# The level products of an HGRN2 chunk in one core's kernel: f32 operands, or 16-bit heads and remainders

## What is computed

```python
b = jnp.cumsum(gc, axis=1)                       # gc = log f, per key channel
diff = b[:, :, None] - b[:, None, :]
dec = jnp.where(mask, jnp.exp(jnp.where(mask, diff, 0.0)), 0.0)
A = jnp.einsum('bthk,btshk,bshk->bhts', qc, dec, kc)
o = (jnp.einsum('bhts,bshv->bthv', A, vc)
     + jnp.einsum('bthk,bhkv->bthv', qc * jnp.exp(b), S))
bl = b[:, -1]
S = (jnp.exp(bl)[..., None] * S
     + jnp.einsum('bshk,bshv->bhkv', kc * jnp.exp(bl[:, None] - b), vc))
```

## Time and profile before

| | |
|---|---|
| median of 3 runs | 1023.69 us (1023.05 to 1025.93) |
| the profiled execution: span, first to last instruction | 1026.3 us |
| PE, weight loads, DVE, ACT, POOL busy | 984.2, 714.3, 582.0, 430.0, 161.0 us |
| level products (L462, L464, L469), PE busy | 16.9, 80.4, 10.9 + 7.1 us |
| mean granted clock of PE | 0.981 |

### The profile page before, as it was taken

How to read it: one execution, slowest core, us unless ns; L and a number is a source line. 1 busy time by engine, 2 the same in 40 slices (tenths; PEclk the granted TensorE clock), 3 DMA queues, 4 the chain that set the end, 5 groups by cost and what they waited for, 6 DMA issues and landing times.

```text
span 1026.3 us, 19994 instructions
## 1 busy us (share of the span) xinstructions
PE 984.2 (96%) x7423; PEld 714.3 (70%) x7478; DVE 582.0 (57%) x1652; ACT 430.0 (42%) x810; POOL 161.0 (16%) x208
## 2 busy tenths in 40 slices
PE   7899986899999999999999999999999999999987
PEld 3465875469775887579766976697759775887554
DVE  1453688436763576436754566366635773477445
ACT  2531747313651365135713373237413661345321
POOL 4000024301130112011110112011301130111212
PEclk9999998899999999999999999999999999999998
DMA  9984301100110011000110011001101010100413
GB/s 313 326 275 130 118 24 59 62 2 21 42 63 0 20 41 43 19 20 0 42 62 0 21 41 62 0 21 41 62 0 41 0 50 1 42 1 23 118 42 111
DMA packets 46590, 60.62 MB, mean 59 GB/s; under 512 B 2748, under 2 KB 40208, under 8 KB 46524
## 3 DMA queue, kind: packets, MB, share of 16 engines
q1 hardware_dynamic: 46524, 59.86, 17.8%
HBM read 48.90 MB, written 10.95 MB: 58 GB/s over the span
## 4 chain that ended last, share of the span: by engine, by line
PE 90%; DVE 5%; issue 2%; ACT 1%; DMA 1%; SPq 1%; DVEq 0%; ACTq 0%
PE ring L390 66%; PE lev L464 7%; PE aux L507 3%; PE okv L521 2%; PE lev L469 1%; PE okv L491 1%; PE lev L462 1%; PE ring L521 1%; PE okv L493 1%; PE okv L492 1%; DMA work<-in_w_in_dram 1%; PE okv L811 1%; PE aux L441 1%; PE aux L477 1%; PE aux L428 1%
## 5 line engine op out<-in xcount | busy, mean ns | idle before, releaser
L390 PE MATMUL ring<-hnh,wih 128*128 128x256 bf16 (+1 forms) x1152 | 291.1, 264 | 5.8 <-DVE hnl L1273 4.2
L390 PE MATMUL ring<-hnh,wil 128*128 128x256 bf16 (+1 forms) x1152 | 291.2, 264 | 0.0
L390 PE MATMUL ring<-hnl,wih 128*128 128x256 f16 (+1 forms) x1152 | 291.1, 264 | 0.0
L390 PE MATMUL ring<-woh,work 128*128 128x512 f16 x512 | 162.3, 379 | 1.7
L390 PEld LDWEIGHTS ring<-hnh,wih 128*128 128x128 f16 x1152 | 112.5, 100 | 18.1 <-issue 4.5
L1165 DVE TENSOR_TENSOR qq<-qq,gg 128x256 f32<-128x256 f32 x96 | 44.1, 459 | 140.1 <-PE lev L464 99.8
L390 PEld LDWEIGHTS ring<-hnl,wih 128*128 128x128 f16 x1152 | 110.6, 98 | 12.9
L390 PEld LDWEIGHTS ring<-hnh,wil 128*128 128x128 bf16 x1152 | 110.6, 98 | 12.4
L390 PE MATMUL ring<-wih,hnh 128*128 128x512 f16 (+1 forms) x264 | 101.1, 383 | 4.0 <-ACT kk L851 4.0
L390 PE MATMUL ring<-wih,hnl 128*128 128x512 f16 (+1 forms) x264 | 101.1, 383 | 1.4 <-issue 0.2
L1587 POOL TENSOR_TENSOR kk<-kk,cols 128x256 f32<-128x256 f32 x32 | 29.3, 935 | 419.3 <-ACT kk L851 419.3
(11 more groups left out here) (310 smaller groups left out, 1585.5 us busy)
## 6 DMA issues: line engine op xcount, KB each, us to landing
xin<-in_x_prompt_dram SPq DMA_DIRECT2D x16, 512.0 KB, 3.4
work<-in_x_prompt_dram SPq DMA_DIRECT2D x16, 512.0 KB, 4.3
out_dram<-work SPq DMA_DIRECT2D x16, 512.0 KB, 2.6
work<-in_ada_w_dram SPq DMA_DIRECT2D x4, 1024.0 KB, 10.4
woh<-in_ada_w_dram SPq DMA_DIRECT2D x4, 1024.0 KB, 11.8
work<-in_w_in_dram SPq DMA_DIRECT2D x4, 1024.0 KB, 7.2
woh<-in_w_in_dram SPq DMA_DIRECT2D x4, 1024.0 KB, 8.5
wol<-in_w_in_dram SPq DMA_DIRECT2D x4, 1024.0 KB, 9.6
```

The costliest lines, as they stand in the source:

```text
L390: last = mm(out, a(k), b(k), start=start and k == ks[0] and j == 0, stop=stop and k == ks[-1] and j == 2)
```

## The change

Queries and keys of every level are split as the projections' operands are, and `level` makes three 16-bit products per block: key head with query head, key head with query remainder, key remainder with query head. It does this at all levels in full width, so levels 6 and 7 no longer work in small blocks. The head of q and k is made by ACT (`q_out` for level 0, `k_head`, and `heads` for the others), the remainder of q by DVE (`operands`), the remainder of k by POOL (`k_rest`). The updates of q, k and the decays are now `carry`, and `take` only copies a level into `am`. There are two sets of operands, so those of level l are made once level l-2 is through PE; `operands(l)`, `take(l - 2)` and `carry(l)` follow each other on DVE. Only the blocks that a level changes are split again: 256 of 512 columns. The decode stage keeps its f32 products.

```diff
+        qrh, qrl = sb("qrh", [P, 2 * T], BF16), sb("qrl", [P, 2 * T], F16)
+        qhi = [sb(f"qhi{i}", [P, T], BF16) for i in range(2)]
+        qlo = [sb(f"qlo{i}", [P, T], F16) for i in range(2)]
+        khi = [sb(f"khi{i}", [P, 2 * T], F16) for i in range(2)]
+        klo = [sb(f"klo{i}", [P, 2 * T], BF16) for i in range(2)]
...
+        def k_set(l):
+            return max(l - 1, 0) % 2
+
+        def odd(t, l):
+            return blocks(t, 1 << (l - 1))[:, :, 1, :]
+
+        def even(t, l):
+            return blocks(t, 1 << (l - 1))[:, :, 0, :]
+
+        def packed(t, l):
+            return t.rearrange("p (b m) -> p b m", m=1 << (l - 1))
...
-                if l == 0:
-                    pe.wait_ge(q_sb.sem, q_sb.at(n, p + 1))
-                    pe.wait_ge(k_ok.sem, k_ok.at(n, 2 * p + 2))
-                elif l == 1:
-                    pe.wait_ge(q_f.sem, q_f.at(n, p + 1))
-                else:
-                    pe.wait_ge(q_upd.sem, q_upd.at(n, LEVELS * p + l - 1))
-                    pe.wait_ge(k_upd.sem, k_upd.at(n, LEVELS * p + l - 1))
-                m = 1 << (l - 1) if l else 0
+                pe.wait_ge(q_lo.sem, q_lo.at(n, i + 1))
+                pe.wait_ge(k_lo.sem, k_lo.at(n, LEVELS * p + max(l, 1)))
+                kh, kl = khi[k_set(l)], klo[k_set(l)]
+                qh, ql, w = (qrh, qrl, P) if l == 0 else (qhi[l % 2], qlo[l % 2], P // 2)
                 for hc in range(4):
-                    q, k = qq[:, P * hc:P * hc + P], kk[:, P * hc:P * hc + P]
-                    if l == 0:
-                        last = mm(lev[i % 2][:, P * hc:P * hc + P], k, q, start=True, stop=True)
-                    elif m < 32:
-                        last = mm(lev[i % 2][:, P // 2 * hc:P // 2 * hc + P // 2], k, blocks(q, m)[:, :, 1, :],
-                                  start=True, stop=True)
-                    else:
-                        for s in range(0, P, 2 * m):
-                            o = P // 2 * hc + s // 2
-                            last = mm(lev[i % 2][s:s + m, o:o + m], k[:, s:s + m], q[:, s + m:s + 2 * m],
-                                      start=True, stop=True)
+                    o, a, b = lev[i % 2][:, w * hc:w * hc + w], slice(P * hc, P * hc + P), slice(w * hc, w * hc + w)
+                    mm(o, kh[:, a], qh[:, b], start=True, stop=False)
+                    mm(o, kh[:, a], ql[:, b], start=False, stop=False)
+                    last = mm(o, kl[:, a], qh[:, b], start=False, stop=True)
                 last.then_inc(lev_ps.sem, 1)
...
             def q_out(n, p):
                 act.wait_ge(q_ps.sem, q_ps.at(n, p + 1))
+                A(qrh[:, :], ring[1][:, :], ACT.Copy).then_inc(q_hi.sem, 1)
                 A(qq[:, :], ring[1][:, :], ACT.Copy).then_inc(q_sb.sem, 1)
+
+            def k_head(n, p):
+                act.wait_ge(k_ok.sem, k_ok.at(n, 2 * p + 2))
+                A(khi[0][:, :], kk[:, :], ACT.Copy).then_inc(k_hi.sem, 1)
+
+            def heads(n, p, l):
+
+                if l >= 3:
+                    act.wait_ge(lev_ps.sem, lev_ps.at(n, p * (LEVELS + 1) + l - 1))
+                if l >= 2:
+                    act.wait_ge(k_upd.sem, k_upd.at(n, LEVELS * p + l - 1))
+                    A(even(khi[k_set(l)][:, :], l), even(kk[:, :], l), ACT.Copy).then_inc(k_hi.sem, 1)
+                    act.wait_ge(q_upd.sem, q_upd.at(n, LEVELS * p + l - 1))
+                else:
+                    act.wait_ge(q_f.sem, q_f.at(n, p + 1))
+                A(packed(qhi[l % 2][:, :], l), odd(qq[:, :], l), ACT.Copy).then_inc(q_hi.sem, 1)
...
+                k_head(n, 0)
                 q_out(n, 0)
                 weights("wi", 4)
+                heads(n, 0, 1)
+                heads(n, 0, 2)
                 for t in range(NT):
                     act.wait_ge(iv_ps.sem, iv_ps.at(n, t + 1))
                     A(vv[:, t, :], ring[t][:, :], ACT.Copy).then_inc(v_sb.sem, 1)
                     if t == 0:
                         weights("wi", 5)
+                    heads(n, 0, 3 + t)
+                heads(n, 0, 5)
...
+                    if t == 0:
+                        heads(n, 0, 6)
+                        heads(n, 0, 7)
...
+                k_head(n, 1)
                 q_out(n, 1)
                 weights("wi", 9, 10)
+                heads(n, 1, 1)
+                heads(n, 1, 2)
...
                 xa_out(n, 0)
                 weights("wi", 11)
+                heads(n, 1, 3)
                 ga_out(n, 0)
+                heads(n, 1, 4)
+                heads(n, 1, 5)
                 gates_out(n, 0)
                 weights("wo", 0)
                 xa_out(n, 1)
+                heads(n, 1, 6)
                 decay(n, 0)
+                heads(n, 1, 7)
                 root(n, 0)
                 ga_out(n, 1)
...
-            def take(n, p, l):
+            def level_done(n, p, l):
 
                 i = p * (LEVELS + 1) + l
                 dve.wait_ge(lev_ps.sem, lev_ps.at(n, i + 1))
+                if l:
+                    dve.wait_ge(amask.sem, amask.at(n, i))
+
+            def operands(n, p, l):
+
+                dve.wait_ge(q_hi.sem, q_hi.at(n, p * (LEVELS + 1) + l + 1))
                 if l == 0:
                     dve.wait_ge(u_ps.sem, u_ps.at(n, 2 * p))
+                    dve.wait_ge(q_sb.sem, q_sb.at(n, p + 1))
+                    V.tensor_tensor(qrl[:, :], qq[:, :], qrh[:, :], ALU.subtract).then_inc(q_lo.sem, 1)
                     dve.wait_ge(f_ok.sem, f_ok.at(n, p + 1))
                     V.tensor_tensor(qq[:, :], qq[:, :], ff[:, :], ALU.mult).then_inc(q_f.sem, 1)
-                    V.copy_predicated(am[:, :, :], eye[:, :].unsqueeze(1).to_broadcast([P, 4, P]),
-                                      lev[i % 2][:, :].rearrange("p (h t) -> p h t", h=4)).then_inc(amask.sem, 1)
                     return
-                dve.wait_ge(amask.sem, amask.at(n, i))
+                if l >= 2:
+                    level_done(n, p, l - 2)
+                V.tensor_tensor(packed(qlo[l % 2][:, :], l), odd(qq[:, :], l), packed(qhi[l % 2][:, :], l), ALU.subtract)\
+                    .then_inc(q_lo.sem, 1)
+
+            def carry(n, p, l):
+
                 m = 1 << (l - 1)
                 nb = 2 * T // (2 * m)
                 j = LEVELS * p + l
@@ -1158,14 +1212,26 @@
                     dve.wait_ge(q_f.sem, q_f.at(n, p + 1))
                 else:
                     dve.wait_ge(q_upd.sem, q_upd.at(n, j - 1))
-                    dve.wait_ge(k_upd.sem, k_upd.at(n, j - 1))
                     dve.wait_ge(g_upd.sem, g_upd.at(n, j - 1))
+                dve.wait_ge(q_lo.sem, q_lo.at(n, p * (LEVELS + 1) + l + 1))
                 g = products(m)
-                qo, ke = blocks(qq[:, :], m)[:, :, 1, :], blocks(kk[:, :], m)[:, :, 0, :]
+                qo, ke = odd(qq[:, :], l), even(kk[:, :], l)
                 V.tensor_tensor(qo, qo, g[:, :, 0:1].to_broadcast([P, nb, m]), ALU.mult).then_inc(q_upd.sem, 1)
+                dve.wait_ge(k_lo.sem, k_lo.at(n, j))
                 V.tensor_tensor(ke, ke, g[:, :, 1:2].to_broadcast([P, nb, m]), ALU.mult).then_inc(k_upd.sem, 1)
+                if p == 0 and l == LEVELS:
+                    level_done(n, 0, LEVELS - 1)
                 o = goff(2 * m)
                 V.tensor_tensor(gg[:, o:o + nb], g[:, :, 0], g[:, :, 1], ALU.mult).then_inc(g_upd.sem, 1)
+
+            def take(n, p, l):
+
+                i = p * (LEVELS + 1) + l
+                if l == 0:
+                    V.copy_predicated(am[:, :, :], eye[:, :].unsqueeze(1).to_broadcast([P, 4, P]),
+                                      lev[i % 2][:, :].rearrange("p (h t) -> p h t", h=4)).then_inc(amask.sem, 1)
+                    return
+                m = 1 << (l - 1)
                 r = m if m == P // 2 else P
...
+                operands(n, 0, 0)
                 if not first:
                     y_rest(n - 1, 0)
+                operands(n, 0, 1)
+                carry(n, 0, 1)
+                if not first:
                     y_rest(n - 1, 1)
-                    y_split(n - 1)
-                for l in range(LEVELS + 1):
-                    take(n, 0, l)
-                    if l == 0:
+                for l in range(2, LEVELS + 1):
+                    operands(n, 0, l)
+                    take(n, 0, l - 2)
+                    carry(n, 0, l)
+                    if l == 2:
                         weights(5)
+                        if not first:
+                            y_split(n - 1)
+                take(n, 0, LEVELS - 1)
+                level_done(n, 0, LEVELS)
+                if not first:
+                    m_out(n - 1, 0)
+                take(n, 0, LEVELS)
                 weights(6)
-                if not first:
-                    m_out(n - 1, 0)
                 state(n, 0, 0)
                 if not first:
                     m_out(n - 1, 1)
@@ -1339,11 +1415,18 @@
                     x_out(n - 1, 0)
                 forget(n, 1)
                 weights(9, 10)
```

(56 more changed lines are left out.)

12 lines of the change are left out of this document (10 added, 2 removed).

## The result

| | before | changed |
|---|---|---|
| median, 4 runs each on one chip | 1024.7 us (1023.05 to 1025.93) | 1037.43 us (1036.43 to 1040.0) |
| profiled execution, span | 1026.3 us | 1034.7 us |
| a middle body (first forget-gate product to the next) | 108.43 us | 109.19 us |
| first product of the second body | 186.38 | 194.54 |
| first product of the decode stage | 935.93 | 944.14 |

The ratio is 1.0123, with a 95% interval from 1.0103 to 1.0143: slower, by 12.7 us in the medians.

What follows compares the result with a forecast made beforehand. PE was taken to bound the kernel, busy 96% of the span. -50.4 (levels) + 14.0 (level 0 wait) + 18.9 (second gates wait) + 11.9 (clock) + 7.9 (first body) = +2.3 us, giving 1026 us; range 986 to 1046.

Steps and rivals of the forecast that it cites:

- Rival 3: Slower: the clock falls at level 0 and the second gates, strided POOL remainders at 0.9 us; 1041 us, chance 0.24.
- The levels: PE's twelve products take 0.35 us a level, 0.67 at level 0; saves 3.15 us a half, 50.4 over 16.
- the bound above it: Upper bound on PE's product cost, a straight line between two rows: 37 ns at 64 columns, 62 at 128.
- The first place: Level 0 at a body's start: PE waits 2.0 us for q's remainder on DVE; seven bodies, 14.0 us.
- the walk from the earlier trace: Stepping POOL, DVE and PE through a body's start in the old profile, giving the 2.0 us wait at level 0.
- The second place: Gates of the second half: PE waits 2.7 us for DVE's second convolution; seven bodies, 18.9 us.
- The clock: PE's granted clock falls after the 2.7 us gates wait, costing 1.7 us a body, 11.9 us in all.
- the 1.68 us wait in the earlier trace: Idle row in the old profile; Rival 3 decides once the level 0 wait passes it, for 2.0 is more.
- Rival 2: The waits come but the clock stays up: 1014 us, from 1004 to 1021; chance 0.20.
- The first body: Body with weight pieces and no y_head: takes back 7.9 us (4 to 12) of the saving.
- Rival 1: Waits hardly come, 1.5 us a body, with no fall of the clock: 989 us, 975 to 1004; chance 0.22.

Runs made afterwards that it cites:

- e7_one: Changed kernel, loop kept, with only the first of each level's three products (head times head), so A lacks the remainder products: 1021.62 us, one run.
- e2_unrolled: Changed kernel with all eight bodies written out on every engine, no loop: 1023.06 us, ratio 0.9956 to the kernel before.
- e5_hn: Changed kernel, loop kept, with ACT's normalised blocks and DVE's remainders and second convolution earlier, take 7 last: 1014.61 us, ratio 0.9881 to the kernel before.
- e1_conv: Changed kernel with the second convolution moved directly behind recur(0) on DVE: 1036.33 us, ratio 1.0101 to the kernel before.
- e4_gp: Changed kernel with ACT's first-body copy of the modulation gate moved ahead of the heads of levels 1 and 2: 1037.11 us, ratio 1.0109 to the kernel before.
- e8_two: Changed kernel, loop kept, with two of each level's three products (the one with the remainder of k left out): 1037.93 us, one run.
- e6_all: Kernel of e5_hn with all bodies written out and the first body's gate copy moved forward: 998.02 us, ratio 0.9715 to the kernel before.
- e10: Kernel of e6_all with ACT's ga_out(1) back ahead of hn_out(1), directly behind the root: 1001.48 us, ratio 0.9766 to the kernel before.

## Why the prediction was right in its range and wrong in its sum

Forecast was +2.3 us of span; it is +8.4. The terms, as measured in the profiled execution:

| term | forecast | measured |
|---|---|---|
| PE's levels | -50.4 | 3.15 a half, 16 halves: -50.4 |
| wait at level 0 | +14.0 | 0 |
| idle time at the loop's start | not seen | 5 x 2.13 = +10.7 |
| wait before the second gates | +18.9 | 6 x 2.89 + 2.13 = +19.5 |
| wait before level 5 | not seen | 6 x 0.43 = +2.6 |
| clock | +11.9 | 7 falls x 1.7 = +11.9 |
| first body beyond the saving | +7.9 | 8.16 + 6.3 = +14.5 |
| sum | +2.3 | +8.8 (8.4 by the spans) |

That the time still lies in the range is in part luck: a term of +14.0 that did not come stands against terms of +10.7, +2.6 and +6.6 that were missing or too small. The measured 1037.4 us is nearer to Rival 3's 1041 than to the forecast's 1026, although the wait at level 0, on which Rival 3 rests, did not come, and POOL's strided remainders took 0.76 us and not its 0.9.

**The levels** were right to the hundredth: 0.35 and 0.67 us for twelve products, or 29 ns a product of 64 columns and 56 ns one of 128. The estimate from the decode rows held, and not the bound above it, 37 and 62 ns.

**The first place** failed as a sum, not as a mechanism. In the body read above the hold is there, in DVE's and POOL's timeline:

```profile
417.84 2.01 POOL L1667 TENSOR_TENSOR work<-sil,stat 128x1024 bf16<-128x1024 f32 x1
418.01 2.38 DVE L1197 TENSOR_TENSOR qrl<-qq,qrh 128x512 f16<-128x512 f32 x1
```

The remainder is there at 420.39, and PE reaches level 0 at 420.60: 0.21 us to spare, because PE itself had lost 1.9 us at the loop's start. In e7_one, where PE does not lose them and DVE still does, the wait is 1.6 to 2.0 us in all five bodies behind a jump. Nor is the hold there every time: of the changed kernel's seven bodies it is in three (2.38 us); in the other four the remainder starts first and takes 0.68, as it does in each body of e2_unrolled, where neither engine loses time at a jump and nothing waits. So the step that failed is the walk from the earlier trace rows, which took PE's start and DVE's start in the old trace as fixed to one another: DVE's own 1.8 to 2.0 us at the jump were in it, PE's new ones were not. It also took one body, behind a jump, for all seven. The scan was held too, for which the prediction had no row: the two scans took 1.63 us beside POOL's bounds (305.73) and 2.17 beside `klo` (414.86), against 1.39 in the earlier trace rows; and the remainder took 2.38 beside y_head against 0.68.

**The loop's start** was in no case of mine. It could have been suspected from the trace of before: in five bodies DVE idled 1.8 to 2.0 us at the jump, released by "issue", and q8 had moved 27 packets in all and none from 295 to 829 us, that is in the loop behind its first turn; the change adds 120 matmuls to a loop of 712. The prediction counted what a product costs, and not how many the loop holds.

**The second place** was right, step and size: 2.73 us against 2.7. The chain was also the right one to attack: e5_hn, which takes ACT's first two normalised blocks and DVE's convolution forward in their queues, won 23 us.

**The clock** was right in sum, seven falls of 1.7 us, by luck: its reason was not. The 1.7 us that the prediction counts for a fall is what the window behind the 1.68 us wait in the earlier trace rows has lost, 6.00 x (1 - 0.72) = 1.68 us; the changed kernel's seven falls lasted 3.41 us at 0.50 each, 1.7 us again. I had tied it to the gates' wait alone, one fall each; it fell behind four of the six waits of 2.73 us, behind the one of 1.96 in the last body, and behind two of the five at the jump. The same count over the runs, from the second body on and without the last: behind a wait of 2.2 to 3.05 us before the gates or `turn_k` (the changed kernel, e1, e2, e4, e7, e8) the clock fell 29 times in 36; behind the 1.8 to 2.3 us at the jump 9 times in 30; behind a wait of 1.0 to 1.3 us (e5, e6, e10) never in 18. Nor did it fall behind the five waits of 1.64 to 1.98 us before level 0 in e7_one. So the 1.68 us of the earlier trace rows was a fair warning of a chance, not a threshold. Why e2_unrolled had only two falls behind six waits of 2.98 us is open. The falls at both level 0 and the gates of Rival 3 came in no body of the changed kernel, since level 0 did not wait; and Rival 2's clock that stays up was not seen either, each of its middle bodies holds one fall.

**The first body** was mis-sized by 6.6 us. The first half saves nothing (109.28 against 109.36 at the first product of its second half), where I had -1.4. In the second half I had 3.0 us of DVE work; PE's waits there (us):

```profile
126.94 0.29 PE L476 MATMUL lev<-qrh,khi 128*128 128x128 bf16 x1 [5.22 <-ACT gp L1040]
...
149.31 0.24 PE L476 MATMUL lev<-qhi,khi 128*128 128x64 bf16 x1 [2.99 <-DVE am L1239]
...
165.78 1.11 PE L485 MATMUL aux<-ident,kk 128*128 128x128 f32 x4 [9.56 <-DVE hnl L1339]
171.11 3.78 PE L515 MATMUL aux<-xc,wg 128*128 128x256 f32 x8 [4.21 <-DVE xc L1299]
```

The first is one that a reader of the diff could find: ACT's copy of the modulation gate, which frees the `lev` banks, had come to stand behind heads that wait for DVE. e4_gp took 3.9 us of it away and the body gave 2.8 back. How the rest divides between weight pieces, splits and the low clock was not tried.

**Rival 1**, that the waits hardly come, described what the change could be with another order of the queues and no loop: e6_all, at 998 us, lies in its range.

## What to carry to other kernels

A change that takes work off the engine that bounds the kernel is worth what the next engines' queues let through; here the same products are worth +12.7 us or -28.6 us by the order of five items on two engines and the form of the loop. Count the instructions that are added to a loop on each engine, and look in the profile for packets of the instruction queue and for idle time released by "issue" at the jump: here PE had neither in a middle body with 704 and 712 matmuls, and with 768 and 832 it had 9 packets and 1.8 to 2.3 us. When a wait is moved, look at the instruction in front of the one that waited: it may want the same thing.

## What the hardware showed that was not expected

- With a loop of 712 matmuls on TensorE (the kernel before) q8 moved no packet in a middle body; with one of 768 (e8_two) it moved 9, 0.15 MB, and TensorE stood still for 2.0 to 2.2 us at the jump, in four of five bodies with 1.1 to 1.5 us more behind it. The straight code here had no such idle time: the longest one released by "issue" there was 0.7 us (e1_conv, decode stage). Why the longer loop's instructions are moved in every turn and the shorter one's are not, no run shows.
- VectorE had 1.76 to 2.15 us of idle time at the jump of its loop in every kernel with a loop, the one before too, and none in those without.
- With 16-bit operands and one weight load per product, a product took 56 ns at 128 columns and 29 ns at 64 (0.67 us for level 0's twelve, 0.35 for another level's, from starts in the changed kernel).
- The same GpSimd and VectorE pair of operations came out in two orders from body to body: either the remainder of q took 0.68 us and the product behind it 2.38, or the remainder 2.38 and the product 0.68. The one that started first had its way: VectorE's at 309.86 us before GpSimd's y_head at 309.95, GpSimd's at 417.84 before VectorE's at 418.01. Which of the two is held decides over a wait on TensorE.
